# Routing of a product-key expert layer: one comparison for both key halves on VectorE, multiplication and addition to expert numbers on GpSimd

## The reference, cut to what matters

```
q = (h @ wq).reshape(Bb, S, PEER_HEADS, 2, PEER_HALF)
s1 = einsum('bshd,hnd->bshn', q[..., 0, :], sub_k1)
s2 = einsum('bshd,hnd->bshn', q[..., 1, :], sub_k2)
v1, i1 = lax.top_k(s1, PEER_TOPK)
v2, i2 = lax.top_k(s2, PEER_TOPK)
cand_s = (v1[..., :, None] + v2[..., None, :]).reshape(..., 256)
cand_e = (i1[..., :, None] * PEER_N_KEYS + i2[..., None, :]).reshape(..., 256)
top_s, pos = lax.top_k(cand_s, PEER_TOPK)
experts = take_along_axis(cand_e, pos, axis=-1)
g = softmax(top_s)
```

## Time and profile before

| what | value |
|---|---|
| time of the runs, median of 3 | 2772.47 us (2768.51 to 2774.18) |
| profiled execution: span from first to last instruction | 2769.1 us |
| profiled execution: time around its span | not shown on its own; the median of the runs is 3.4 us above the span |
| busy in the profiled execution | PE 1889.1, DVE 1874.9, POOL 1083.9, ACT 404.5 us |
| bytes moved | 850.48 MB, mean 307 GB/s |
| gathers' queue | 538.17 MB |

### The profile page before, as it was taken

One profiled execution on the slowest core, in us unless ns is written; L12 is line 12 of the kernel. 1 busy time (PEld: TensorE's weight loads), 2 busy tenths in 40 slices (PEclk: granted clock), 3 DMA queues, 4 the chain that ended last, 5 costly groups with the idle time before them and its releaser, 6 DMA issues.

```text
span 2769.1 us, 24483 instructions
## 1 busy us (share of the span) xinstructions
PE 1889.1 (68%) x8517; PEld 1371.7 (50%) x8517; DVE 1874.9 (68%) x3412; ACT 404.5 (15%) x904; POOL 1083.9 (39%) x1059
## 2 busy tenths in 40 slices
PE   7988444276654363544535546689439999999998
PEld 5786111265443161134333145564237887478873
DVE  2758998889578979988889997676974342242001
ACT  1321001122103020012111010000104100041000
POOL 2004435577256555755566765555640000000000
PEclk8999555596676675967767878889759999999999
DMA  9629999999899999999999989999963693422443
GB/s 342 226 80 375 399 395 400 332 377 378 324 397 404 399 401 401 350 332 405 404 397 389 358 313 394 392 391 409 354 243 107 218 299 125 163 93 92 152 152 121
DMA packets 357626, 850.48 MB, mean 307 GB/s; under 512 B 23832, under 2 KB 147072, under 8 KB 357376
## 3 DMA queue, kind: packets, MB, share of 16 engines
q0 software_dynamic: 148672, 538.17, 50.7%
q1 hardware_dynamic: 208832, 310.76, 32.1%
HBM read 847.79 MB, written 1.05 MB: 307 GB/s over the span
## 4 chain that ended last, share of the span: by engine, by line
PE 37%; DMA 32%; DVE 14%; issue 11%; POOL 3%; ACT 2%; SPq 1%; DVEq 0%; POOLq 0%; ACTq 0%
PE bank L1137 13%; DMA RING<-in_peer_v,EX 7%; PE bank L1167 6%; DMA W<-in_w_ada 5%; DMA W<-in_ada_w 4%; PE bank L453 3%; DMA RING<-in_peer_u,EX 3%; DMA W<-in_w_gate 3%; DMA WORK<-in_peer_u,EX 3%; DMA W<-in_w_up 3%; PE bank L462 2%; POOL RING L1295 2%; PE bank L1081 2%; DVE ACC L2032 2%; DMA WORK<-in_peer_v,EX 2%
## 5 line engine op out<-in xcount | busy, mean ns | idle before, releaser
L1137 PE MATMUL bank<-HT,W 128*128 128x256 f32 x1984 | 457.5, 395 | 59.9 <-DMA W<-in_w_gate 30.8
L1295 POOL DMA_INDIRECT RING<-in_peer_u,EX x343 | 327.4, 955 | 355.9 <-DVE ACC L2014 224.3
L2014 DVE SCALAR_TENSOR_TENSOR ACC<-RING,hrows 128x1024 bf16<-128x1024 f32 x343 | 407.2, 1218 | 86.1 <-DMA RING<-in_peer_u,EX 80.1
L1295 POOL DMA_INDIRECT RING<-in_peer_v,EX x341 | 382.7, 1122 | 197.1 <-issue 76.4
L1137 PEld LDWEIGHTS bank<-HT,W 128*128 128x128 f32 x1984 | 392.7, 199 | 123.9 <-DMA W<-in_w_gate 34.0
L490 PE MATMUL bank<-W,CACT 128*32 128x512 f32 x544 | 117.1, 959 | 200.1 <-DMA W<-in_w_ada 117.3
L1295 POOL DMA_INDIRECT WORK<-in_peer_v,EX x171 | 196.1, 1147 | 103.0 <-DVE hrows L2032 45.7
L1167 PE MATMUL bank<-W,WORK 128*128 128x512 f32 x528 | 230.2, 599 | 2.4 <-DVE WORK L2716 2.4
L1295 POOL DMA_INDIRECT WORK<-in_peer_u,EX x169 | 160.4, 949 | 168.1 <-DVE ACC L2014 145.7
L2014 DVE SCALAR_TENSOR_TENSOR ACC<-WORK,hrows 128x1024 bf16<-128x1024 f32 x169 | 201.4, 1218 | 33.9 <-DMA WORK<-in_peer_u,EX 33.3
L2032 DVE SCALAR_TENSOR_TENSOR ACC<-RING,ACTS,ACC 128x1024 f32<-128x1024 f32 x155 | 198.5, 1281 | 27.1 <-DMA RING<-in_peer_v,EX 26.6
(11 more groups left out here) (434 smaller groups left out, 2826.1 us busy)
## 6 DMA issues: line engine op xcount, KB each, us to landing
W<-in_ada_w SPq DMA_DIRECT2D x36, 1024.0 KB, 11.7
W<-in_w_gate SPq DMA_DIRECT2D x33, 1024.0 KB, 7.7
W<-in_w_up SPq DMA_DIRECT2D x33, 1024.0 KB, 5.5
W<-in_w_down SPq DMA_DIRECT2D x33, 1024.0 KB, 5.0
W<-in_w_in SPq DMA_DIRECT2D x32, 1024.0 KB, 16.5
W<-in_w_ada SPq DMA_DIRECT2D x32, 1024.0 KB, 17.2
W<-in_peer_wq SPq DMA_DIRECT2D x24, 1024.0 KB, 18.2
W<-in_w_o SPq DMA_DIRECT2D x10, 1024.0 KB, 15.6
```

Source lines behind the costliest of these rows:

```text
L1137: mm = pe.matmul(bs[j][:, g * S:(g + 1) * S], w[:, k, j * P:(j + 1) * P], HT[:, k, :], start=(k == 0 and g == 0), stop=(k == DC - 1 and g ...
L1295: gp.indirect_dma_start(SLOT[g % NS], None, rows, bass.IndirectOffsetOnAxis(EX[:, t, k:k + 1], 0))\
L2014: ve.scalar_tensor_tensor(out=JUNK[:, g % 2, :], in0=SLOT[g % NS], scalar=1.0, in1=HB[:, :], op0=ALU.mult, op1=ALU.mult, accum_out=ACTS[:, ...
```

## The change

VectorE's fourth step of a group now also turns the key numbers into the two terms of the expert number: `TIF` of the first half is key times 128 plus the layer's offset, of the second half the key itself. After the places are split it makes one comparison over both halves (two heads, two halves, 16 picks, 16 places: 1024 elements for each partition) into `EQ`, which grows from 512 to 1024 columns, and raises a new mark `picked`. The fifth step is empty, except for the first group of all, whose numbers VectorE works out itself. For the other fifteen, GpSimd waits for `picked`, multiplies `EQ` with `TIF` (1024), adds the second half to the first (512), adds halves of the 16 places to each other (256, 128, 64, 32), and copies the result into `EX` as whole numbers (32), with a wait on its own semaphore between any two. GpSimd does that ahead of the gather into the slot that the first row of the round after the fourth step gives back (`NUMBERED_AT`). The mark `routed` is now one semaphore for all groups. VectorE waits, before it writes the single buffers again, for the numbers of the group before; ScalarE's wait and one at the head of the context block are for the same mark. Some semaphores are merged (`ident_in` into `consts_in`, `x_loaded` and `stored` into `x_moved`). `stepper` moves up, unchanged.

```
-        EQ = carve(11392, GP * TOPK)
+        EQ = carve(11392, 2 * GP * TOPK).rearrange("p (u k a) -> p u k a", u=GSETS, k=TOPK)
...
+        ROUTE_STEPS = 5
+        FIRST_STEPS = [1 + k % 2 for k in range(PICKS // 4)]
+        LATER_ROUNDS = [8 + (23 * i) // 20 for i in range(ROUTE_STEPS * GROUPS)]
+
+        def round_of_first(step):
+
+            return next(k for k in range(len(FIRST_STEPS)) if sum(FIRST_STEPS[:k + 1]) > step)
+
+        NUMBERED_AT = {}
+        for i_, (t_, g_) in enumerate([(0, g) for g in range(1, GROUPS)] + [(1, g) for g in range(GROUPS)]):
+            NUMBERED_AT[gather(0, 0, 0, 4 * (round_of_first(ROUTE_STEPS * i_ + 3) + 1)) + NS] = (0, t_, g_)
+        for t_, g_ in itertools.product(range(NT), range(GROUPS)):
+            NUMBERED_AT[gather(t_, 1 - t_, 1, 4 * (LATER_ROUNDS[ROUTE_STEPS * g_ + 3] + 1)) + NS] = (1, t_, g_)
...
+        def expert_numbers(eng, do, settle, l, t, g):
+
+            do(eng.tensor_tensor(EQ, EQ, TIF.unsqueeze(2).to_broadcast([P, GSETS, TOPK, TOPK]), ALU.mult))
+            settle()
+            eq = EQ.rearrange("p (h e) k a -> p h e k a", e=2)
+            part = eq[:, :, 0, :, :]
+            do(eng.tensor_tensor(part, part, eq[:, :, 1, :, :], ALU.add))
+            width = TOPK
+            while width > 1:
+                width //= 2
+                settle()
+                do(eng.tensor_tensor(part[:, :, :, 0:width], part[:, :, :, 0:width], part[:, :, :, width:2 * width], ALU.add))
+            settle()
+            do(eng.tensor_copy(EX[:, t, g * GP:(g + 1) * GP].rearrange("p (h k) -> p h k", h=GHEADS), part[:, :, :, 0]),
+               mark("routed", "all"))
...
                             g = gather(l, t, table, k)
+                            if g in NUMBERED_AT:
+                                lg, tg, group = NUMBERED_AT[g]
+                                gp.wait_ge(mark("picked", "all"), groups_routed(lg, tg, group) + 1)
+                                expert_numbers(gp, do, settle, lg, tg, group)
                             if table == 0 and k % GP == 0:
-                                gp.wait_ge(mark("routed", f"b{l}"), t * GROUPS + k // GP + 1)
+                                gp.wait_ge(mark("routed", "all"), groups_routed(l, t, k // GP) + 1)
...
-                    act.wait_ge(mark("routed", p), t * GROUPS)
+                    act.wait_ge(mark("routed", "all"), groups_routed(l, t, 0))
...
-                do(ve.tensor_copy(TIF, TI))
...
-                bp = BP.rearrange("p h k -> p (h k)")
-                do(ve.tensor_scalar(BQ[:, 0, :], bp, 4, None, ALU.logical_shift_right))
-                do(ve.tensor_scalar(BQ[:, 1, :], bp, TOPK - 1, None, ALU.bitwise_and))
-                settle()
-                do(ve.tensor_copy(BF, BQ))
+                n = groups_routed(l, t, g)
+                if n:
+                    ve.wait_ge(mark("routed", "all"), n)
+                tif = TIF.rearrange("p (h e) k -> p h e k", e=2)
+                ti = TI.rearrange("p (h e) k -> p h e k", e=2)
+                do(ve.tensor_scalar(tif[:, :, 0, :], ti[:, :, 0, :], float(KEYS), float(l * EXPERTS), ALU.mult, ALU.add))
+                do(ve.tensor_copy(tif[:, :, 1, :], ti[:, :, 1, :]))
+                do(ve.tensor_scalar(BQ[:, :, 0, :], BP, 4, None, ALU.logical_shift_right))
+                do(ve.tensor_scalar(BQ[:, :, 1, :], BP, TOPK - 1, None, ALU.bitwise_and))
+                settle()
+                do(ve.tensor_copy(BF.rearrange("p (h e) k -> p h e k", e=2), BQ))
...
                 settle()
+                where = [P, GSETS, TOPK, TOPK]
+                do(ve.tensor_tensor(EQ, BF.unsqueeze(3).to_broadcast(where),
+                                    const("iota").unsqueeze(1).unsqueeze(1).to_broadcast(where), ALU.is_equal), mark("picked", "all"))
                 yield
-                tif = TIF.rearrange("p (h e) k -> p h e k", e=2)
-                eq = EQ.rearrange("p (h k a) -> p h k a", h=GHEADS, k=TOPK)
-                eqn = EQ.rearrange("p (n a) -> p n a", a=TOPK)
-                for e in range(2):
-                    do(ve.tensor_tensor(eqn, BF[:, e, :].unsqueeze(2).to_broadcast([P, GP, TOPK]),
-                                        const("iota").unsqueeze(1).to_broadcast([P, GP, TOPK]), ALU.is_equal))
-                    settle()
-                    do(ve.tensor_tensor(eq, eq, tif[:, :, e, :].unsqueeze(2).to_broadcast(full), ALU.mult))
-                    settle()
-                    do(ve.tensor_reduce(EF[:, e, :], eqn, AX.X, ALU.add))
-                    settle()
-                do(ve.scalar_tensor_tensor(out=EF[:, 0, :], in0=EF[:, 0, :], scalar=float(KEYS), in1=EF[:, 1, :],
-                                           op0=ALU.mult, op1=ALU.add))
-                settle()
-                do(ve.tensor_scalar(EX[:, t, picks], EF[:, 0, :], float(l * EXPERTS), None, ALU.add), mark("routed", p))
+                if n == 0:
+                    settle()
+                    expert_numbers(ve, do, settle, l, t, g)
                 yield
...
+                if p == "c0":
+                    ve.wait_ge(mark("routed", "all"), groups_routed(1, 0, 0))
```

More of the change, by code:

```diff
@@ L201, in network @@
         BP = carve(12640, GP).bitcast(u32).rearrange("p (h k) -> p h k", h=GHEADS)
[L202 to L204 removed]
+        BQ = carve(12672, 2 * GP).bitcast(u32).rearrange("p (h e k) -> p h e k", h=GHEADS, e=2)
+        BF = carve(12736, 2 * GP).rearrange("p (u k) -> p u k", u=GSETS)
         V1B = carve(0, 1024).rearrange("p (t h n) -> p t h n", t=NT, h=H1)
@@ L271, in network @@
         w_passed = sem("w_passed")
-        v_step, a_step = sem("v_step"), sem("a_step")
-        ident_in, consts_in, conditions = sem("ident_in"), sem("consts_in"), sem("conditions")
-        x_loaded, ctx_loaded = sem("x_loaded"), sem("ctx_loaded")
+        v_step, a_step, p_step = sem("v_step"), sem("a_step"), sem("p_step")
+        consts_in, conditions = sem("consts_in"), sem("conditions")
+        x_moved, ctx_loaded = sem("x_moved"), sem("ctx_loaded")
         vectors = sem("vectors")
@@ L311, in vector_done, with groups_routed @@
             return sum(1 for w_, _ in freed_by[:g] if w_ == "V")
+        ROUTE_STEPS = 5
[8 more added lines that the diff above has]
+            NUMBERED_AT[gather(t_, 1 - t_, 1, 4 * (LATER_ROUNDS[ROUTE_STEPS * g_ + 3] + 1)) + NS] = (1, t_, g_)
+        def groups_routed(l, t, g):
+            return (l * NT + t) * GROUPS + g
+        def expert_numbers(eng, do, settle, l, t, g):
[12 more added lines that the diff above has]
+               mark("routed", "all"))
         def place(n):
@@ L580, in block1 @@
                             mm.then_inc(filled, 1)
-                pe.wait_ge(consts_in, 16)
+                pe.wait_ge(consts_in, 16 * 2)
                 vectors_1 = ada_steps(p, aw, [0], GATE1)
@@ L1190, in block2 @@
                             last_read(mm, c == NF // 2 - 1 and banks["dn", p, 1, 1][0] + 1, e)
-            pe.wait_ge(ident_in, 16)
+            pe.wait_ge(consts_in, 16)
             pe.wait_ge(conditions, 16 * 3)
@@ L1230, in _ @@
             early = CONST["who"][1]
-            sp.dma_start(K_[:, 0:early], d["consts"][:, 0:early]).then_inc(ident_in, 16)
+            sp.dma_start(K_[:, 0:early], d["consts"][:, 0:early]).then_inc(consts_in, 16)
             sp.wait_ge(mark("cleared", "all"), 1)
@@ L1255, in _, with stepper, do, settle @@
                 sp.wait_ge(mark("xu", "l1"), NT + t + 1)
-                sp.dma_start(out[0, t * P:(t + 1) * P, :], X[:, t, :]).then_inc(stored, 16)
-            sp.wait_ge(stored, 16 * NT)
+                sp.dma_start(out[0, t * P:(t + 1) * P, :], X[:, t, :]).then_inc(x_moved, 16)
+            sp.wait_ge(x_moved, 16 * (NT + 1))
+        def stepper(eng, chain):
+            n, last = {}, [None]
+            def do(ins, s=chain):
+                n[s.name] = n.get(s.name, 0) + 1
+                ins.then_inc(s, 1)
+                last[0] = (s, n[s.name])
+            def settle():
+                eng.wait_ge(*last[0])
+            return do, settle, n
         @block.gpsimd
@@ L1281, in _ @@
                 gp.dma_start(SKN[:, :, e, :], keys[0].rearrange("h n d -> n h d")).then_inc(mark("skn", "b0"), 16)
+            do, settle, _ = stepper(gp, p_step)
             for l in range(LAYERS):
@@ L1298, in network @@
         MODS = {"b0": 0, "b1": 0, "c0": 1, "c1": 1, "l0": 2, "l1": 3}
[L1300 to L1312, removed]
         def two(ap):
@@ L1904, in angles @@
             def angles():
-                ve.wait_ge(consts_in, 16)
+                ve.wait_ge(consts_in, 16 * 2)
                 ve.wait_ge(vectors, 16 * 17)
@@ L2240, in block1 @@
                 if l == 0:
-                    ve.wait_ge(x_loaded, 16)
+                    ve.wait_ge(x_moved, 16)
                 normalise(p, 1, X, LN_EPS, False, XN, mark("y", p))
@@ L2421, in gate @@
                     yield
-                every = {k: [choices] * (1 + k % 2) for k in range(ROUNDS)}
```

(3 more changed lines are left out.)

3 lines of the change are left out of this document (1 added, 2 removed).

## The result

The changed kernel takes 2813.7 us (2810.83 to 2815.63) beside 2773.3 of the kernel before: a ratio of 1.0147, 95% interval 1.0131 to 1.0164, some 40 us slower. The forecast was 2793: the direction and the range hold, the size is half of what came.

The account below looks back on a forecast made before the run. VectorE looked like the bound in the second halves of S1 and S2, POOL nearly as full and taking over. 0 + 5.0 + 10.2 + 5.2 = +20.4 us on 2769.1, plus 3.4 kept: 2793, range 2768 to 2830.

Parts of the forecast that it names:

- What bounds the kernel: VectorE looks like the bound in the second halves of S1 and S2, 98% busy, with POOL nearly as full.
- S1: Stage with four routing groups beside the sums of (layer 0, tile 1); first interval 0, second and third +5.0 us.
- S2: Stage with four routing groups beside the sums of (layer 1, tile 0); its three intervals were forecast at +10.2 us.
- VectorE's busy time: Sign to look for over the whole execution: it should fall by some 48 us, 3.2 us a group over fifteen groups.
- The intervals: Spans between ends of groups' fourth steps in S1 and S2; gathers times 1.38 us plus 6.6 a group: 0, +5.0, +10.2.
- T: POOL's arithmetic per group: VectorE's durations 3.2, seven steps of 0.30 us 2.1, meeting with sums 1.3; together 6.6 us.
- The tails: From the fourth group's fourth step to the last sum, in S1 and S2: 18.4 us for 15.8, +2.6 us, twice.
- S0: Stage with seven routing groups beside the dots of (layer 0, tile 0); gain at most 6, loss at most 12, taken 0.
- Rival B: POOL's arithmetic collides with two-SBUF-input sums, each of seven operations waiting half a sum: 9.8 us a group, 2815; chance 0.22.
- Rivals C and D: C: POOL just fits, 4.2 us a group, 2772, chance 0.17. D: VectorE stays the bound in S1 and S2, 2749, 0.14.

Follow-up runs that it names:

- first_stage_only: Changed kernel, but GpSimd makes only the numbers of the seven groups beside S0's dots, VectorE the rest: 1.0032 against the kernel before, +9 us.
- vector_numbers: Changed kernel, but VectorE makes the numbers of all sixteen groups and GpSimd only gathers: 0.9986 against the kernel before, -4 us.
- the two holds: first_stage_only, with GpSimd's first gathers of the next sums and of the following dots waiting for adaLN weight chunks: 1.0002 against the kernel before, +1 us.

## Why the prediction was right in direction and short in size

- **What bounds the kernel**: right. POOL was nearly full in the second halves of S1 and S2, and with the arithmetic it became the bound; VectorE idles 25 us in S2's second half before rows that have just landed. That VectorE's busy time fell by 34 and not 48 us is mostly the held sums: 10 us more in the sums into ACC over the whole execution (307.3 in place of 297.2).
- **The intervals**: the formula (gathers by pitch, plus groups by T, GpSimd's time for one group) was right, and its pitch nearly so (1.38 taken, 1.34 measured; POOL's gathers waited 1.2 us for other engines from pick to pick, as forecast). S1's second and third interval were forecast at +5.0 and came at +5.6; S2 at +10.2 and came at +12.8; the first interval, at 0, at +0.6. That S1 came so close is partly luck: a T that was too small and a pitch that was too long offset each other.
- **T, the term "3.2 + 2.1 + 1.3 = 6.6 us"**: mis-sized, 8.4 us in S2 and 6.2 in S0. All three of its parts were off, two of them against each other. VectorE's durations were too short for POOL: 2.35 us for 1024 elements (1.22 taken), 1.27 for 512 (0.69), 0.72 for 256 (0.42), 5.55 in all seven and not 3.2. POOL's step of 0.30 us is a step of gathers; between dependent operations it is 0.08, six times 0.08 = 0.5 and not 2.1. And the meeting with sums costs 7.95 - 5.55 = 2.4 and not 1.3. The rule of the Trainium skill that the prediction cited and did not take (GPSIMD Engine Reference, "Performance versus the Vector engine", a factor of 1.96) is nearer to the rows: 2.35 / 1.22 = 1.93 for the 1024, though 1.7 for the 256.
- **The tails**: +2.6 each taken, +4.8 and +3.9 came. T is in them too. With the intervals this is 27.7 against 20.4 us, 7 of the 19 us that are missing.
- **S0, "I take 0"**: the step that failed most: 9.4 of the missing 19 us lie ahead of S1's first pick, and first_stage_only has +9 us. The prediction had the mechanism as the upper end of this term (nine slots' rows fetched ahead of the weights that the gelu waits for, 12 us), and took 0, between that loss and a gain of 6, without a row for it. The chain of the earlier trace rows already showed that the weights end the stage, so that dots which end earlier could only send rows in front of them. The loss (+13 against vector_numbers) is gone with the two holds. The remaining 3 us lie in neither place, and their cause stays open.
- **Rival B** was half right, and more than it was given: the arithmetic does meet the sums, and without the meeting 16 us come back. Its price by "half a sum for each of seven operations" was not how it goes: the short ones mostly fit between two meetings (in S2 the 128, the 32 and the copy kept their durations), and two or three in a group are hit there, the 512 and the 256 in every one. Its sentence that no row shows a sum held is answered by the sum of 3.20 us.
- **Rivals C and D** fell: they needed 4.2 and 3.1 us of arithmetic, and POOL alone needs 6. VectorE's saving came to nothing everywhere: in S0 the weights were the end, in S1 and S2 POOL.

## What to carry to other kernels

Price work that is moved to another engine by that engine's own rows, and ask first how full its queue is where the work lands: here a us of arithmetic on GpSimd's queue came back about seven times in S1 and S2 when the meeting with the sums was taken out (16 us for 2.4) and about nine times when work was added (25 for 2.7). Look at which buffers lie in SBUF on both sides; one accumulator moved to PSUM for twelve rows gave 16 us. And where a stage ends with a transfer, as S0 does with its weights, work that gets faster ahead of it fetches the next stage's data into that transfer's time: hold the fetch until the transfer has passed.

## What the runs showed of the hardware that was not expected

- GpSimd's dependent elementwise operations follow each other after 0.08 us, while its gathers are 0.30 us apart; the smallest took 0.23 to 0.29 us (a copy of 32 elements 228 ns, an addition of 32 244, of 64 292).
- A sum of VectorE with two SBUF inputs was held up by one operation of GpSimd: it took 3.20 us in place of 1.27, begun 0.24 us into a multiplication of 2.35.
- No effect of the other traffic on GpSimd's arithmetic shows: beside DMA at 398 GB/s and VectorE's dots, which have one input in SBUF and one in PSUM, the 512 took 1267 ns, and beside sums with one input in SBUF 1264. Of S0's seven multiplications six took 2.35 us; the seventh took 3.27, begun 0.17 us into an operation of VectorE on two inputs in SBUF (L2285, 353.04).
